# The front of a one-core transformer layer rebuilt: projections, state-space scan, heads and mix in another order and on other engines

## The reference

```python
h = rms_norm(x, norm1_g)                         # 256 x 1024
proj = h @ w_in                                  # 1024 x 2816, split in
ua, qb, kb, vb, qc, kc, vc, gc = split(proj)     # 256, 3 x 512, 4 x 256 columns
ya = rms_unit(s5_mixer(ua))      # bu = u @ B; complex linear scan over time, 1024 states;
                                 # y = re(C state) + u*d; y = gelu(y); y = y*sigmoid(y @ w_glu)
yb = rms_unit(moba_mixer(qb, kb, vb))            # per head rms norm and rope of q and k,
                                                 # causal softmax attention, 8 heads of 64
yc = silu(gc) * rms_unit(retention(qc, kc, vc))  # rotary, decayed scores, 4 heads of 64
x = x + (concat(ya, yb, yc) * mix_out_g) @ w_out # 1024 x 1024
h2 = rms_norm(x, norm2_g)
x = x + peer_layer(h2)           # h2 @ w_q, scores against keys, top-k of 16384 experts,
                                 # gelu(h2 @ u^T) weighted by the gates, times v
```

## Time and profile before

| | |
|---|---|
| median of three runs | 970.44 us |
| profiled execution, its own time | 970.3 us |
| its span, first to last instruction | 968.5 us |
| TensorE busy over the span | 926.8 us (96%) |
| VectorE, ScalarE, GpSimd busy | 692.5, 528.8, 447.8 us |
| first product by `w_out` starts | 154.86 us |
| last product by `w_out` ends, empty products start | 176.71 us |
| first product by `w_q` starts | 186.66 us |

### The profile page before, as it was taken

How to read it: one execution, slowest core, us unless ns; L and a number is a source line. 1 busy time by engine, 2 the same in 40 slices (tenths; PEclk the granted TensorE clock), 3 DMA queues, 4 the chain that set the end, 5 groups by cost and what they waited for, 6 DMA issues and landing times.

```text
span 968.5 us, 20031 instructions
## 1 busy us (share of the span) xinstructions
PE 926.8 (96%) x5920; PEld 828.8 (86%) x5920; DVE 692.5 (72%) x1496; ACT 528.8 (55%) x1044; POOL 447.8 (46%) x370
## 2 busy tenths in 40 slices
PE   5794999999999999999999999999999999999998
PEld 5553568899999999999999999988888888888886
DVE  7379534202999912688888887788888888888886
ACT  4622555555555455555555555655566555655553
POOL 1779606587888888777777777300000000000000
PEclk9897999999999999999999999999999999999999
DMA  9422222216666666565555555776767677777773
GB/s 332 160 104 87 87 87 90 108 45 217 200 231 225 230 230 208 206 199 194 193 196 194 200 190 194 234 245 239 247 238 243 231 246 236 248 238 244 243 234 134
DMA packets 67435, 191.45 MB, mean 198 GB/s; under 512 B 6480, under 2 KB 8272, under 8 KB 67408
## 3 DMA queue, kind: packets, MB, share of 16 engines
q1 hardware_dynamic: 67408, 191.11, 57.8%
HBM read 173.78 MB, written 17.30 MB: 197 GB/s over the span
## 4 chain that ended last, share of the span: by engine, by line
PE 70%; POOL 14%; issue 7%; DVE 5%; ACT 3%; DMA 0%; POOLq 0%; SPq 0%; DVEq 0%
PE ps L426 21%; PE ps L427 21%; PE ps L428 21%; POOL w_lo L1455 10%; PE ps L666 3%; POOL w_lo L1419 2%; DVE routing L737 2%; PE ps L408 1%; PE ps L521 1%; ACT w_hi L1147 1%; PE ps L392 1%; ACT h_hi L1154 0%; DMA xs<-in_x 0%; DVE small L737 0%; DVE route_t L737 0%
## 5 line engine op out<-in xcount | busy, mean ns | idle before, releaser
L1311 ACT ACTIVATE w_hi<-raw 128x512 fp32r<-128x512 f32 x512 | 308.4, 628 | 137.3 <-PE ps L428 136.2
L1455 POOL TENSOR_TENSOR w_lo<-raw,w_hi 128x512 fp32r<-128x512 f32 x256 | 327.0, 1298 | 81.2 <-ACT w_hi L1311 80.9
L426 PE MATMUL ps<-h_hi,w_hi 128*128 128x256 f32 x1088 | 308.5, 284 | 2.5 <-POOL w_lo L1455 1.1
L427 PE MATMUL ps<-h_lo,w_hi 128*128 128x256 f32 x1088 | 307.9, 283 | 0.0
L428 PE MATMUL ps<-h_hi,w_lo 128*128 128x256 f32 x1088 | 307.8, 283 | 0.0
L737 DVE TENSOR_TENSOR w_lo<-raw,w_hi 128x512 fp32r<-128x512 f32 x256 | 177.4, 693 | 56.9 <-ACT w_hi L1311 41.9
L426 PEld LDWEIGHTS ps<-h_hi,w_hi 128*128 128x128 f32 x1088 | 208.8, 192 | 3.3 <-POOL w_lo L1455 1.3
L427 PEld LDWEIGHTS ps<-h_lo,w_hi 128*128 128x128 f32 x1088 | 208.8, 192 | 0.0
L428 PEld LDWEIGHTS ps<-h_hi,w_lo 128*128 128x128 f32 x1088 | 208.8, 192 | 0.0
L426 PE MATMUL ps<-w_hi,hot_gate 128*128 128x512 f32 x512 | 199.2, 389 | 0.0
L427 PE MATMUL ps<-w_lo,hot_gate 128*128 128x512 f32 x512 | 199.2, 389 | 0.0
(11 more groups left out here) (196 smaller groups left out, 885.2 us busy)
## 6 DMA issues: line engine op xcount, KB each, us to landing
raw<-in_u_t SPq DMA_DIRECT2D x128, 512.0 KB, 3.4
raw<-in_v SPq DMA_DIRECT2D x128, 512.0 KB, 3.4
act_spill<-acts SPq DMA_DIRECT2D x62, 256.0 KB, 2.1
acts<-act_spill SPq DMA_DIRECT2D x62, 256.0 KB, 3.4
routing<-in_w_in SPq DMA_DIRECT2D x5, 2048.0 KB, 9.3
routing<-in_w_out SPq DMA_DIRECT2D x2, 2048.0 KB, 8.2
routing<-in_w_q SPq DMA_DIRECT2D x2, 2048.0 KB, 7.7
xs<-in_x SPq DMA_DIRECT2D x2, 512.0 KB, 4.9
```

The costliest lines, as they stand in the source:

```text
L426: pe.matmul(dst, s_hi, m_hi, start=first and i == 0, stop=False)
L427: pe.matmul(dst, s_hi, m_lo, start=False, stop=False)
L1311: A.activation(w_hi[:, 2 * (s % 2) + h, :], raw[:, s, h * HALF:(h + 1) * HALF], ACT.Copy)\
L1455: G.tensor_tensor(w_lo[:, slot, :], raw[:, s, h * HALF:(h + 1) * HALF], w_hi[:, slot, :].bitcast(F32), ALU.subtract).then_inc(lo_ready, 1)
```

## The change

- `w_in` piece 0 is multiplied natively in fp32: ScalarE and VectorE write the transposed `h` (4 tiles each) into `hT` in full precision, 16 products of 256 columns follow; `h_hi` is rounded from `hT` (`rounded`), and `h_lo` is made by GpSimd. Its weights come as two transfers, and the identity and the time steps as two.
- Pieces 1 to 5 are all multiplied in halves (40 slices); `project` is gone. The retention's q and k come third, its v and gate fourth.
- The state-space part runs in four quarters (`states(n)`, 2 x 256 time steps): the turned drive and the scans stay in PSUM, and each quarter's `drive(n)` waits for the states of the quarter before. The 32 products with C go round the four column groups.
- Norm, scale and rope of q and k, and the retention's rotation, move from GpSimd to VectorE (`heads`, `rotate`). GpSimd is left with the low halves.
- q and k are transposed apart; the scores of the later 128 tokens come in two parts, with masks, maxima and exponentials in two parts as well.
- y, its gelu, the gate and the mix come after the attention's products. The gates are formed from `ACT.Tanh` (constants folded into the norms). ScalarE squares from PSUM, and the roots use separate places of `std`.
- `ymix` is complete in three steps (`ret_mix`, `moba_mix`, `s5_mix`), transposed in three steps, and `w_out` is multiplied in the order of `MIX_ORDER`, the state-space rows last.
- Before the second norm, ScalarE takes the root and `xn` first and the high halves of the first `w_q` slices afterwards.

```diff
+MIX_ORDER = (6, 7, 2, 3, 4, 5, 0, 1)
...
+            first = w_src[0].rearrange("(k p) n -> p k n", p=P)
+            sp.dma_start(w_ring[0][:, 0:4, 0:S5_CH], first[:, 0:4]).then_inc(first_in, 16)
+            sp.dma_start(times, consts[:, C_IOTA:C_N]).then_inc(times_in, 16)
+            sp.dma_start(w_ring[0][:, 4:KC, 0:S5_CH], first[:, 4:KC]).then_inc(w_in_sem[0], 16)
+            sp.dma_start(rawf[:, 2304:2816], s5_b).then_inc(s5_b_in, 16)
+            for n in range(1, W_N):
+                if n == 3:
                     sp.dma_start(rot, rots).then_inc(consts_in, 16)
...
...
+                    sp.wait_ge(u_psum, TT)
+                elif 3 < n <= 8:
+                    sp.wait_ge(lo_ready, KC * (n - W_SLOTS))
+                elif n > 8:
+                    sp.wait_ge(lo_ready, FRONT + KC * (n - W_SLOTS - 5))
+                sp.dma_start(w_ring[n % W_SLOTS], w_src[n].rearrange("(k p) n -> p k n", p=P))\
+                    .then_inc(w_in_sem[n % W_SLOTS], 16)
...
+            def drive(n):
 
                 for r in range(2):
-                    for j in range(4):
-                        mm = pe.matmul(ps[:, 4 + j, r * S:(r + 1) * S],
-                                       bT[32 * j:32 * j + 32, r * 2 + c, :], uT[32 * j:32 * j + 32, c, :],
-                                       start=True, stop=True)
+                    for jj in range(2):
+                        j = 2 * (n % 2) + jj
+                        mm = pe.matmul(ps[:, 6 + jj, r * S:(r + 1) * S], bT[32 * j:32 * j + 32, r * 2 + n // 2, :],
+                                       uT[32 * j:32 * j + 32, n // 2, :], start=True, stop=True)
...
+                pe.wait_ge(full_act if k < 4 else full_dve, k % 4 + 1)
+                for t in range(TT):
+                    mm = pe.matmul(ps[:, 4 + 3 * t, 0:S5_CH], hT[:, k, t * P:(t + 1) * P], w_ring[0][:, k, 0:S5_CH],
+                                   start=(k == 0), stop=(k == KC - 1))
+                    if k == KC - 1:
+                        mm.then_inc(u_psum, 1)
...
+            by_slices(1, range(0, 1))
...
+            by_slices(1, range(1, 3))
             pe.wait_ge(u_ready, 1)
             pe.wait_ge(bT_ready, 1)
             drive(0)
...
+            by_slices(1, range(3, KC))
+            by_slices(2, range(0, 3))
+            pe.wait_ge(states_ready, 1)
             drive(1)
...
+            by_slices(2, range(3, KC))
+            turn_heads(0)
+            by_slices(3, range(0, 6))
+            pe.wait_ge(states_ready, 2)
+            drive(2)
+            by_slices(3, range(6, KC))
+            by_slices(4, range(0, 2))
+            turn_heads(1)
+            by_slices(4, range(2, 4))
+            late_scores(0)
+            by_slices(4, range(4, 6))
+            late_scores(1)
+            by_slices(4, range(6, KC))
...
+            by_slices(5, range(0, 3))
...
+            by_slices(5, range(3, KC))
+            pe.wait_ge(states_ready, 3)
+            drive(3)
...
+                signs = ((c_s[:, 0], pc), (c_neg[:, 0], zb), (c_neg[:, 1], xr), (c_neg[:, 1], pS))
+                for n, (w, st) in enumerate(signs):
+                    for j in range(4):
+                        mm = pe.matmul(ps[32 * j:32 * j + 32, 6, c * S:(c + 1) * S], w[:, 4 * c + j, :], st[:, 4 * c + j],
+                                       start=(n == 0), stop=(n == len(signs) - 1))
...
+            keep_warm(ident, 7, 8)
+            pe.wait_ge(ret_mix, 1)
+            transpose_mix(MIX_ORDER[0:2])
+            pe.wait_ge(moba_mix, 1)
+            transpose_mix(MIX_ORDER[2:6])
             for n in range(2):
-                for k in range(KC):
+                for i, k in enumerate(MIX_ORDER):
                     if n == 0:
-                        pe.wait_ge(th_ready, KC + k + 1)
-                        pe.wait_ge(tl_ready, KC + k + 1)
-                    pe.wait_ge(lo_ready, FRONT + KC * n + k + 1)
+                        if i == 4:
+                            pe.wait_ge(s5_mix, 1)
+                            transpose_mix(MIX_ORDER[6:8])
+                        pe.wait_ge(th_ready, KC + i + 1)
+                        pe.wait_ge(tl_ready, KC + i + 1)
...
+            def rotate(views):
+                for x1, x2, co, si, ta, tb in views:
+                    did(tt(ta, x2, si, ALU.mult))
+                    did(tt(tb, x1, si, ALU.mult))
+                settle()
...
+            def heads(a):
+                h4 = qk[:, :, a * MW:(a + 1) * MW].rearrange("p t (h d) -> p t h d", d=HD)
+                d_ = slice(16 * a, 16 * a + 16)
                 dve.wait_ge(qk_sq, a + 1)
...
+                n_th = variance(sums[:, d_], 0, 16, 1.0 / HD)
+                for t in range(TT):
+                    did(tt(h4[:, t], h4[:, t], cols(V_GQK + a * HD, HD).unsqueeze(1).to_broadcast([P, MH, HD]), ALU.mult))
+                settle()
+                rstd_of(n_th, 0, 16, qk_rstd[:, d_]).then_inc(qk_rstd_ready, 1)
+                dve.wait_ge(qk_rstd_ready, a + 1)
+                for t in range(TT):
+                    r_v = qk_rstd[:, 16 * a + 8 * t:16 * a + 8 * t + 8].unsqueeze(2).to_broadcast([P, MH, HD])
+                    did(tt(h4[:, t], h4[:, t], r_v, ALU.mult))
+                settle()
+                rotate(rotation(qk[:, :, a * MW:(a + 1) * MW], MH, ROPE // 2, C_RC, C_RS, rot_tmp[:, 1024:2048]))\
+                    .then_inc(rot_ready, 1)
+                dve.wait_ge(rot_ready, a + 1)
+                settle()
+
+            zr_p, zi_p = ps[:, 6:8, 0:S], ps[:, 6:8, S:2 * S]
+
+            def states(n):
+
+                js = slice(2 * n, 2 * n + 2)
+                dve.wait_ge(phase_ready, 2 * (n // 2) + 2)
+                dve.wait_ge(bu_psum, n + 1)
+                did(tt(drive_c, zr_p, pc[:, js], ALU.mult))
+                did(tt(drive_s, zr_p, pS[:, js], ALU.mult))
+                settle()
+                did(tt(zr_p, zi_p, pS[:, js], ALU.mult))
+                settle()
+                did(tt(zi_p, zi_p, pc[:, js], ALU.mult))
+                settle()
+                did(tt(zr_p, zr_p, drive_c, ALU.add))
+                did(tt(zi_p, zi_p, drive_s, ALU.subtract))
+                settle()
+                for jj in range(2):
+                    for z in (zr_p, zi_p):
+                        did(V.tensor_tensor_scan(z[:, jj], mag[:, 2 * n + jj:2 * n + jj + 1].to_broadcast([P, S]), z[:, jj],
+                                                 0.0, ALU.mult, ALU.add))
+                settle()
+                did(tt(xr[:, js], zi_p, pc[:, js], ALU.mult))
+                did(tt(zb[:, js], zi_p, pS[:, js], ALU.mult))
+                settle()
+                did(tt(pc[:, js], zr_p, pc[:, js], ALU.mult))
+                tt(pS[:, js], zr_p, pS[:, js], ALU.mult).then_inc(states_ready, 1)
+                dve.wait_ge(states_ready, n + 1)
+                settle()
+
...
+            states(0)
             dve.wait_ge(consts_in, 80)
+            heads(0)
             V.tensor_scalar(c_neg, c_s, -1.0, None, ALU.mult).then_inc(c_ready, 1)
             dve.wait_ge(c_ready, 1)
...
+            states(1)
+            heads(1)
+            dve.wait_ge(proj_ready, 6)
+            rotate(rotation(ret, 2 * RH, HD // 2, C_TC, C_TS, rot_tmp[:, 1024:2048])).then_inc(ret_rot_ready, 1)
...
+            late_scores(0)
+            late_scores(1)
...
+            states(2)
+            states(3)
...
+            dve.wait_ge(gate_ready, 1)
...
+            V.scalar_tensor_tensor(uT[:], gate_s.rearrange("p (c t) -> p c t", c=S5_C), 1.0, uT[:], ALU.add,
+                                   ALU.mult).then_inc(ya_ready, 1)
...
+            squares_x(0)
+            act.wait_ge(expo_ready, 1)
+            A.activation(mag, expo, ACT.Exp).then_inc(mag_ready, 1)
+            squares_x(1)
+            full(0)
+            full(1)
+            root(TT)
+            full(2)
+            full(3)
+            rounded(range(0, 4))
+            act.wait_ge(ang_ready, 1)
+            did(A.activation(s1, ang, ACT.Sin))
+            settle()
+            A.activation(c1, half, ACT.Sin).then_inc(trig_ready, 1)
+            rounded(range(4, KC))
+            slices_high(range(0, 2))
+            act.wait_ge(rx_ready, 1)
+            act.wait_ge(u_psum, TT)
+            for t in range(TT):
+                A.activation(u_tok[:, t, :], ps[:, 4 + 3 * t, 0:S5_CH], ACT.Copy,
+                             scale=rx[:, t:t + 1]).then_inc(u_tok_ready, 1)
+            slices_high(range(2, 3))
+            act.wait_ge(zeros_ready, 2)
+            phases(0)
+            act.wait_ge(uT_psum, 1)
+            A.activation(uT, ps[:, 5, :].rearrange("p (c t) -> p c t", c=S5_C), ACT.Copy).then_inc(u_ready, 1)
+            slices_high(range(3, 4))
+            act.wait_ge(bT_psum, 1)
+            A.activation(bT, ps[:, 6, :].rearrange("p (a s) -> p a s", a=4), ACT.Copy).then_inc(bT_ready, 1)
+            slices_high(range(4, 5))
+            phases(1)
+            slices_high(range(5, 11))
+            projected(0)
...
```

(14 more changed lines are left out.)

606 lines of the change are left out of this document (258 added, 348 removed).

## The result

The median of the changed kernel is 966.21 us (962.5 to 968.53, seven executions), that of the kernel before, run beside it, 970.44 (970.22 to 974.39). The ratio is 0.9947, 95% interval 0.9926 to 0.9969: faster by 0.5%, and by the medians 4.2 us where 10.4 were forecast. The measured time lies in the range; the gain is less than half of what was said.

A forecast was written before the change was run, and what follows sets the result against it. TensorE bounds the expert loops; VectorE and GpSimd, taking turns, hold up the front. w_out starts 15.2 us earlier, 2.9 + 0.5 + 1.5 are given back, the second norm saves 0.3: -10.6 on 970.3, forecast 960 us, range 949 to 969.

The forecast's parts named there:

- Up to the masks: Front, from the first slice at 20.0 through VectorE's heads and states to the retention's masks, done at 116.3 us.
- turns: Front: each VectorE operation with two SBUF inputs that meets a GpSimd low half waits 0.94 us; 7.0 in q's heads.
- the rival with fewer of them: Front: small operations slip between GpSimd's, so half of the 16.0 us of waits go: 952 us; chance 0.20.
- all 16.0 us of turns: Front: VectorE's waits for GpSimd, 3.4 + 7.0 + 4.6 + 1.0, all claimed to lie on the path.
- the price of the half clock in the tail: Behind the masks: retention's products, 2.6 us, run partly at half clock and take 4.0; transposes 0.9, attention's first products 1.8.
- TensorE is slow in the tail: Tail: y's products stay at 0.25 us, or half clock lasts through retention's and y's products; 964 to 967, chance 0.17.
- The estimate of 6 us: y's 32 products in distinct column groups at 0.19 us each, 6 us in all, giving 961.5; the forecast took 4.5.
- The way from the gate to w_out: Gate's product's end, 132.5, to w_out's first product, 139.7: 7.2 us where 18.7 were, so -11.5.
- The drain: ScalarE's table change: 1.38 us more behind the 1.28 load; not in the forecast, with it the time would be 961.4.
- the stall: w_out: TensorE stands 2.9 us before the fifth slice, behind ScalarE's rounding of the state-space tiles and that slice's halves.
- The second norm: Behind w_out: high halves of 2.08 us leave ScalarE's chain, but 30 empty products last 6.86 us, so only 0.3 saved.
- the median of the runs lies 0.1 above that execution: Last step of the sum: from the profiled execution's 959.7 to the predicted median of 960 us.

The follow-up runs named there:

- pool_waits: Changed kernel with GpSimd waiting for q's rope before the low half of slice 12; median 967.25 us, ratio to the kernel before 0.9935 to 0.9969.
- warm_tail: Changed kernel with 34 empty products ahead of TensorE's wait for the retention's masks; median 960.76 us, ratio to the kernel before 0.9878 to 0.9913.
- y_in_fours: Changed kernel with four of y's products in a row going to one column group, as before; median 969.15 us, ratio 0.9957 to 0.9992.

## What the prediction had right, and which steps failed

**Up to the masks it held.** First slice 19.35 (forecast 20.0), states(0) from 28.98 (29.7) for 9.2 us (9.3), slice 5 at 33.10 (33.7), q's heads 39.99 to 53.78 (42.0 to 55.4), stalls at the transposes 3.47 and 3.35 (3.5 and 4.1), drive(3) at 103.38 (104.3), retention's products at 116.74 (116.3). That the waits in q's heads are turns is shown by pool_waits; the rival with fewer of them falls. Their length is right in part by luck: the heads alone take 7.5 us, not 6.3, and the eight turns 6.3, not 7.0, two errors that mostly cancel. That all 16.0 us of turns lie on the path is not shown: the 6.3 taken out of q's heads came back in k's. One sum ahead of this is slightly off: four times 7.13 is 28.5, not 28.3, which changes nothing behind it.

**What failed first is the price of the half clock in the tail.** The prediction says: "TensorE has idled, so the retention's products, 2.6 us, run partly at half clock: 4.0, to 120.2. Transposes 0.9, attention's first products 1.8." Measured: 5.2, 1.7 and 2.6, together 9.5 instead of 6.7. It saw the cause and gave it 1.4 us; it cost 4.2 here, and 4.1 came back in warm_tail. The rows it rested on the earlier trace rows have half clock for 4.7 and 3.3 us behind idle times of 9.5 and 12.2; behind 8.68 us here it lasted about nine, through everything up to y. Why so much longer is not settled. The rival "TensorE is slow in the tail" (964 to 967, chance 0.17) comes nearest: the median lies in its band. But it had the half clock last through y's products too, or these stay at 0.25 us each; in the profiled execution they ran at full clock, and only in others (4.61 to 5.25 us) did it reach into them. y's products at 3.66 instead of 4.5 gave 0.8 back; y_in_fours shows both orders side by side, 0.11 and 0.26 us each. The estimate of 6 us worked out from the Trainium skill's figure for packed products (TensorE: Matmul & The Clock Gate, Part 3: Packing small matmuls) came out too long for four column groups in turn; the page's figure is for three groups, and no run here tests it. The gate's product ended at 135.42 instead of 132.5: 0.4 from the start of the retention's products, 2.8 from the half clock, less 0.8 for y, and 0.5 that the prediction had rounded away when it gave 123.0 + 4.5 as 127.

**The way from the gate to w_out held**: 7.5 us, forecast 7.2. The forecast has a gap, though: the terms that it names add up to 6.3, and the other 0.9, the root among it, have no price in it, so its nearness is in part luck. Each table load costs its 1.28 and no drain follows, and the forecast had none. The drain that the Trainium skill gives (ScalarE: Activation LUTs, What ACT_TABLE_LOAD costs) is seen in no row here; the measurement decides. That the gates are tanh has no part in it beyond 0.15 us. Which part of the change gave the other 11 no run takes apart. In the kernel before, TensorE's retention products and the rest of attention's stood behind the gate's product, and then 16 empty products:

```profile
139.16 0.33 PE L580 MATMUL ps<-routing 128*128 128x64 f32 x2
...
147.97 3.79 PE L400 MATMUL ps<-con 128*128 128x128 f32 x32
```

Those 8.8 us now stand ahead of the gate's product, and the roots and norms that the prediction credits are a part of the same reordering.

**In w_out** the stall is 2.88 as forecast (2.9). The half clock was forecast at w_out's start, 1.5 us; it came behind the stall instead, 1.9. w_out took 27.0 us, forecast 26.7. The end of w_out: 169.92 where 166.4 were said.

**The second norm** saved 0.5 (0.3); that the empty products swallow the rest was right, and it was worth 1.5 us.

So the profiled execution missed by 963.1 - 959.7 = 3.4: 2.9 before the gate, 0.3 and 0.3 behind it, less 0.2 at the second norm, and 0.1 that has no place. **The other 3.1 is the step "the median of the runs lies 0.1 above that execution".** That was so for the kernel before and not for this one. The changed kernel's tail stands on a clock whose low stretch varies in length: in profiled executions of kernels alike up to there (but for one gate) y's products took 3.66, 4.61, 5.08 and 5.25 us, by how long it lasted, and the retention's products began between 116.74 and 118.69. In the two traces of longer executions (965.73 and 967.15 us) about half of the 4 us lies ahead of the retention's products and half behind them. How the untraced ones divide, the execution of 966.21 among them, is not shown.

## What to carry to other kernels

Where a change leaves TensorE idle for microseconds ahead of a stretch of small products, price that stretch at up to twice its duration, not at a part of it, or fill the idle time. Fill only waits that lie on the path, count an empty product by its row, and let it end before the wait does: the same trick brought 4.1 us in the tail, at most half a microsecond in the early front, and cost 1.5 us behind w_out, where 30 had been one third too many. An engine held back to spare another only moves the wait, if its work has to be made up beside the same neighbour: q's heads lost 6.3 us of turns and k's gained 5.6. And lay a forecast against the spread of executions, not against the one that was profiled, when the change puts the end on such a stretch.
